# Input projection with high and low halves of the activations in one product, and filler products ahead of the experts

## The reference

```
h = layer_norm(x)
for l in range(2):
    z = h @ w_in[l]                       # 2048 -> 5648, cut into 13 slices
    mix = concat(y_a, y_b, y_c, y_d) @ w_out[l]
    h = layer_norm(alpha * h + mix)
    out = sum over e of combine[:, e] * ((silu(h @ w_gate[e]) * (h @ w_up[e])) @ w_down[e])
    h = layer_norm(alpha * h + out)
```

## Time and profile before

| | |
|---|---|
| median of 3 runs (lowest, highest) | 1715.86 us (1712.81, 1719.31) |
| the profiled execution's own time | 1714.94 us |
| its span, first to last instruction | 1713.2 us |
| mean granted TensorE clock | 0.962 |
| busy: TensorE, VectorE, ScalarE, POOL | 1553.8, 945.7, 546.2, 50.2 us |
| HBM read | 539.88 MB, 316 GB/s over the span |

### The profile page before, as it was taken

One profiled execution on the slowest core, in us unless ns is written; L12 is line 12 of the kernel. 1 busy time (PEld: TensorE's weight loads), 2 busy tenths in 40 slices (PEclk: granted clock), 3 DMA queues, 4 the chain that ended last, 5 costly groups with the idle time before them and its releaser, 6 DMA issues.

```text
span 1713.2 us, 38421 instructions
## 1 busy us (share of the span) xinstructions
PE 1553.8 (91%) x16224; PEld 1090.1 (64%) x16224; DVE 945.7 (55%) x1548; ACT 546.2 (32%) x694; POOL 50.2 (3%) x36
## 2 busy tenths in 40 slices
PE   8999999998899999966599999999997999996664
PEld 8999999884444555422299999998743555452221
DVE  7657655647455556623466476566374556652235
ACT  4553543323222222201265544533321222221112
POOL 0004000000000000000000050000000000000000
PEclk9999999999999999988899999999999999998887
DMA  8655556659999999999965555567589999999996
GB/s 296 216 169 191 170 177 223 244 212 383 420 420 421 420 420 421 420 421 420 396 201 185 165 194 178 162 240 294 235 347 420 420 421 421 421 420 420 421 421 250
DMA packets 138709, 543.88 MB, mean 317 GB/s; under 512 B 23012, under 2 KB 26312, under 8 KB 88536
## 3 DMA queue, kind: packets, MB, share of 16 engines
q1 hardware_dynamic: 138196, 541.97, 81.0%
q10 hardware_dynamic: 388, 0.04, 0.0%
HBM read 539.88 MB, written 2.10 MB: 316 GB/s over the span
## 4 chain that ended last, share of the span: by engine, by line
PE 68%; SPq 15%; DMA 10%; DVE 4%; issue 1%; DVEq 1%; ACT 1%; ACTq 0%
PE ps L826 23%; PE ps L1102 11%; PE ps L988 10%; SPq L408 10%; PE ps L1120 6%; PE ps L823 5%; DMA room<-in_w_up_dram 5%; DMA room<-in_w_down_dram 4%; SPq L412 4%; PE ps L1044 3%; PE ps L1059 3%; PE ps L1079 1%; PE ps L1052 1%; DVE room L1160 1%; DVE w_lo L1160 1%
## 5 line engine op out<-in xcount | busy, mean ns | idle before, releaser
L1102 PE MATMUL ps<-room 128*32 128x256 f32 x5344 | 336.4, 408 | 91.9 <-DMA room<-in_w_up_dram 91.5
L1160 DVE TENSOR_TENSOR w_lo<-room,w_hi 128x2048 fp32r<-128x2048 f32 (+1 forms) x121 | 276.2, 2292 | 228.9 <-ACT w_hi L535 228.4
L1102 PEld LDWEIGHTS ps<-room 128*32 128x32 f32 x5344 | 193.0, 116 | 244.6 <-DMA room<-in_w_up_dram 87.6
L826 PE MATMUL ps<-hT_hi,w_hi 128*128 128x256 f32 x1152 | 329.7, 286 | 1.1 <-DVE w_lo L1160 0.7
L826 PE MATMUL ps<-hT_lo,w_hi 128*128 128x256 f32 x1152 | 326.0, 283 | 0.0
L826 PE MATMUL ps<-hT_hi,w_lo 128*128 128x256 f32 x1152 | 325.9, 283 | 0.0
L535 ACT ACTIVATE w_hi<-room 128x2048 fp32r<-128x2048 f32 x120 | 228.0, 1911 | 228.4 <-PE ps L826 101.7
L1160 DVE TENSOR_TENSOR h<-h,ps 128x512 f32<-128x512 f32 (+1 forms) x380 | 241.7, 698 | 13.7 <-PE ps L1059 13.6
L1160 DVE TENSOR_TENSOR room<-room,ps 128x128 f32<-128x128 f32 (+2 forms) x53 | 18.5, 353 | 400.1 <-ACT room L742 396.7
L826 PEld LDWEIGHTS ps<-hT_hi,w_hi 128*128 128x128 f32 x1152 | 220.9, 192 | 4.7 <-issue 2.4
L826 PEld LDWEIGHTS ps<-hT_hi,w_lo 128*128 128x128 f32 x1152 | 221.0, 192 | 0.7 <-issue 0.5
(11 more groups left out here) (254 smaller groups left out, 1650.0 us busy)
## 6 DMA issues: line engine op xcount, KB each, us to landing
room<-in_w_down_dram SPq DMA_DIRECT2D x116, 1024.0 KB, 22.0
room<-in_w_gate_dram SPq DMA_DIRECT2D x114, 1024.0 KB, 25.3
room<-in_w_up_dram SPq DMA_DIRECT2D x114, 1024.0 KB, 26.8
room<-in_w_in_dram SPq DMA_DIRECT2D x88, 1024.0 KB, 5.0
room<-in_w_out_dram SPq DMA_DIRECT2D x32, 1024.0 KB, 5.2
spare<-in_w_gate_dram SPq DMA_DIRECT2D x14, 1024.0 KB, 24.8
spare<-in_w_up_dram SPq DMA_DIRECT2D x14, 1024.0 KB, 26.7
spare<-in_w_down_dram SPq DMA_DIRECT2D x12, 1024.0 KB, 17.9
```

The lines of the kernel that those rows point to most:

```text
L826: last = eng.matmul(ps[:, b + o // 2, (o % 2) * T:(o % 2) * T + T], w_[:, o * P:o * P + P], x_[:, kk, :], start=opens and o % 2 == 0, stop ...
L1102: last = eng.matmul(ps[r0:r0 + BLK, 0, 0:2 * P], xe[:, x0:x0 + BLK], unit_gu(u)[:, :, k, c * P:c * P + P], start=(i == 0 and k == 0), stop ...
L1160: return eng.tensor_tensor(o, a, b, op)
```

## The change

It has three parts.

1. `hT_hi` and `hT_lo` become two halves of one tensor `hT_parts`. In slabs 1, 3, 4, 5, 7, 8 and 9 (`MERGED`) a high weight block meets both halves in one product of 512 columns, and the low weight block meets `hT_hi` in one of 256. Each column block o has a whole bank: the first 256 words hold high by high and low by high, the other 256 the cross term. The slab thus uses banks 0 to 3.

2. For these slabs `evacuate` is replaced by `copy_cross` on ScalarE (four copies of 256 words, the first three after a column block's last product, the fourth after the slab) and `add_cross` on VectorE (four adds of the bank's first half, each freeing a bank). Where there is a SiLU or GELU, `in_place` applies it after the four adds. Slabs 0, 2, 6 and 10 use banks 0 and 1. The first quarter of a slab waits bank by bank; slabs 1, 3 and 7 take blocks 2 and 3 first. Rounds and splits around these steps change places by one quarter at most.

3. The four fillers in each call of `router` become 12 after the first half's router products, 3 after the second half's transposes and 3 after its router products, and the folding products of both halves move to the end. 3 fillers are put ahead of `turn_rows` and 5 behind it.

```diff
-        hT_hi = part("hT_hi", [P, KD, T], arena_at)
-        hT_lo = part("hT_lo", [P, KD, T], arena_at + 16 * 1024)
+        hT_parts = part("hT_parts", [P, 2, KD, T], arena_at)
+        hT_hi, hT_lo = hT_parts[:, 0], hT_parts[:, 1]
...
+                def copy_cross(s, dst, scale=1.0):
+                    for o in range(4):
+                        if o < 3:
+                            eng.wait_ge(o_done.sem, o_done.at(l, 3 * MERGED.index(s) + o + 1))
+                        else:
+                            eng.wait_ge(w_used.sem, w_used.at(l, 4 * s + 4))
+                        eng.activation(dst[:, o * T:o * T + T], ps[:, o, T:2 * T], ACT.Copy, scale=scale
+                                       ).then_inc(cross_copied.sem, 1)
+
+                def in_place(s, dst, func):
+                    eng.wait_ge(bank_free.sem, freed(l, s))
+                    for i in range(2):
+                        eng.activation(dst[:, i * 512:i * 512 + 512], dst[:, i * 512:i * 512 + 512], func
+                                       ).then_inc(z_evac.sem, 1)
...
+                copy_cross(1, r_x)
                 rounds(11, 12)
-                evacuate(1, r_x)
...
-                rounds(25, 28)
-                evacuate(5, c_g, ACT.Silu)
+                rounds(25, 27)
+                copy_cross(5, c_g)
+                rounds(27, 28)
+                in_place(5, c_g, ACT.Silu)
                 rounds(28, 30)
...
                 eng.activation(a_PT, ps[:, 4:8, 0:384], ACT.Copy).then_inc(att_pTs.sem, 1)
-                rounds(34, 36)
-                evacuate(7, r_g, ACT.Gelu_apprx_tanh)
+                rounds(34, 35)
+                copy_cross(7, r_g)
+                rounds(35, 36)
+                in_place(7, r_g, ACT.Gelu_apprx_tanh)
...
-                    if first == 0 and s >= 2:
-                        eng.wait_ge(z_evac.sem, z_evac.at(l, 2 * (s - 2) + 2))
...
+                        order = (2, 3, 0, 1) if q == 0 and s in (1, 3, 7) else range(2 if token_major else 4)
+                        for ks, o in itertools.product(parts, order):
...
+                            if q == 0 and s:
+                                bank = o if token_major or joined else o // 2
+                                if s in (1, 3, 7) and bank < 2:
+                                    eng.wait_ge(z_evac.sem, evacuated(l, s - 1, bank + 1))
+                                elif s > 1:
+                                    before_it = s - 2 if s in (3, 7) else s - 1
+                                    eng.wait_ge(bank_free.sem, freed(l, before_it, bank))
...
+                                if joined:
+                                    c = slice(o * P, o * P + P)
+                                    eng.matmul(ps[:, o, :], hi[:, c], hT_parts[:, :, kk, :], start=opens, stop=False)
+                                    last = eng.matmul(ps[:, o, 0:T], lo[:, c], hT_hi[:, kk, :], start=False, stop=ends)
+                                    continue
...
                 router(0)
+                keep_busy(12, 7)
                 turn_half(1)
-                router(1).then_inc(logits_done.sem, 1)
+                keep_busy(3, 7)
+                router(1)
+                keep_busy(3, 7)
+                fold_router(0)
+                fold_router(1).then_inc(logits_done.sem, 1)
...
+                keep_busy(3, 2)
                 turn_rows(first_rows.sem, first_rows.at(l, 1), first_turned.sem)
+                keep_busy(5, 2)
...
+                def add_cross(s, dst, scale=1.0):
+                    for o in range(4):
+                        eng.wait_ge(cross_copied.sem, cross_copied.at(l, 4 * MERGED.index(s) + o + 1))
+                        sl = dst[:, o * T:o * T + T]
+                        eng.scalar_tensor_tensor(sl, ps[:, o, 0:T], scale, sl, ALU.mult, ALU.add).then_inc(bank_free.sem, 1)
...
                 splits(10, 11)
+                add_cross(1, r_x)
                 eng.wait_ge(exps_ready.sem, exps_ready.at(l, 1))
...
                     eng.reciprocal(c_rs[:, 512 * i:512 * i + 512], c_rs[:, 512 * i:512 * i + 512])
                     splits(26 + i, 27 + i)
+                    if i == 0:
+                        add_cross(5, c_g)
...
-                splits(32, 37)
-
-                eng.wait_ge(z_evac.sem, z_evac.at(l, 16))
+                splits(32, 35)
+                add_cross(7, r_g)
+                splits(35, 37)
+
+                eng.wait_ge(z_evac.sem, evacuated(l, 7))
...
                 splits(37, 39)
+                add_cross(8, b_c)
                 rest_mix(1, 8)
```

More of the change, by code:

```diff
@@ L270, in trunk, with evacuated, freed @@
         hT_rounded, hT_split = signal("hT_rounded", 5), signal("hT_split", 5)
-        z_evac = signal("z_evac", 2 * (N_IN - 1))
+        z_evac = signal("z_evac", 2 * len(EVACUATED))
+        o_done, cross_copied, bank_free = (signal(n, k * len(MERGED)) for n, k in (
+            ("o_done", 3), ("cross_copied", 4), ("bank_free", 4)))
+        def evacuated(l, s, i=2):
+            return z_evac.at(l, 2 * EVACUATED.index(s) + i)
+        def freed(l, s, o=3):
+            return bank_free.at(l, 4 * MERGED.index(s) + o + 1)
         out_first, res_add = signal("out_first", 1), signal("res_add", 2 * N_OUT)
@@ L649, in _ @@
                 last.then_inc(at_ready.sem, 1)
-                rounds(21, 24)
+                rounds(21, 23)
                 eng.wait_ge(u_ready.sem, u_ready.at(l, 1))
-                evacuate(4, a_kT)
+                copy_cross(4, a_kT)
+                rounds(23, 24)
                 eng.wait_ge(om_ready.sem, om_ready.at(l, 1))
@@ L695, in _ @@
                 rounds(41, 43)
-                evacuate(9, b_h)
+                copy_cross(9, b_h)
                 rounds(43, 47)
@@ L819, in project @@
                                 hi, lo = w_hi[n % 4][:, k, :], w_lo[n % UNITS][:, k, :]
+                                opens, ends = kk == 0, kk == KD - 1
+                                if joined:
[3 more added lines that the diff above has]
+                                    continue
                                 for j, (x_, w_) in enumerate(((hT_hi, hi), (hT_hi, lo), (hT_lo, hi))):
[L821 to L824, removed]
+                                    if token_major:
+                                        last = eng.matmul(ps[:, o, :], x_[:, kk, o * P:o * P + P], w_,
+                                                          start=opens and j == 0, stop=ends and j == 2)
                                     else:
-                                        last = eng.matmul(ps[:, b + o // 2, (o % 2) * T:(o % 2) * T + T],
+                                        last = eng.matmul(ps[:, o // 2, (o % 2) * T:(o % 2) * T + T],
                                                           w_[:, o * P:o * P + P], x_[:, kk, :],
-                                                          start=opens and o % 2 == 0, stop=ends and o % 2 == 1)
+                                                          start=opens and j == 0 and o % 2 == 0,
+                                                          stop=ends and j == 2 and o % 2 == 1)
+                            if joined and q == 3 and o < 3:
+                                last.then_inc(o_done.sem, 1)
                             if between and (q, o) in between:
@@ L921, in _ @@
                 eng.wait_ge(rs_done.sem, rs_done.at(l, 1))
-                eng.wait_ge(z_evac.sem, z_evac.at(l, 10))
+                eng.wait_ge(bank_free.sem, freed(l, 4))
                 qT, kT = blocks(a_qT, 4), blocks(a_kT, 4)
@@ L976, in _ @@
                     if c == 0:
-                        eng.wait_ge(z_evac.sem, z_evac.at(l, 2 * (N_IN - 1)))
+                        eng.wait_ge(bank_free.sem, freed(l, 9))
                     elif c >= 2:
@@ L1336, in _ @@
                     softplus()
-                splits(18, 21)
+                splits(18, 19)
+                add_cross(3, a_qT, float(P) ** -0.5)
+                splits(19, 21)
                 eng.wait_ge(at_ready.sem, at_ready.at(l, 1))
@@ L1417, in _ @@
                 rest_mix(2, 0)
-                splits(41, 44)
-                eng.wait_ge(z_evac.sem, z_evac.at(l, 20))
+                splits(41, 43)
+                add_cross(9, b_h)
+                splits(43, 44)
+                eng.drain()
                 eng.wait_ge(att_o.sem, att_o.at(l, 1))
```

25 lines of the change are left out of this document (15 added, 10 removed).

## The result

| | before | after |
|---|---|---|
| median of 4 runs (lowest, highest) | 1716.78 us (1712.81, 1719.31) | 1774.78 us (1772.23, 1775.92) |
| profiled execution: own time, span | 1714.94, 1713.2 us | 1772.23, 1770.5 us |
| mean granted TensorE clock | 0.962 | 0.947 |
| busy: TensorE, VectorE, ScalarE, POOL | 1553.8, 945.7, 546.2, 50.2 us | 1567.9, 962.4, 553.9, 50.8 us |
| HBM read | 316 GB/s over the span | 306 GB/s over the span |

The change makes the kernel slower: ratio 1.0338, interval 1.0324 to 1.0351. The forecast was 1772 us.

A forecast was written before the change was run, and what follows sets the result against it. TensorE was taken to bound the kernel up to the router, the expert-weight stream after the first gate/up product. 1714.9 + 54.4 - 11.9 - 3.7 + 17.6 = 1771.3, as a median 1772 us; range 1746 to 1787, chance 0.68.

The forecast's parts named there:

- The bound: Projections of both layers: TensorE's own time bounds them, so a microsecond lost or won there is one of the total.
- Rival (4): Expert weight stream: transfers run ahead while TensorE waits and hide the delay; total about 1711 us; chance 0.03.
- The waits: Projections: TensorE waits for banks before slabs 2, 6, 7, 8 and 9; 27.2 us a layer, +54.4 us.
- The two prices taken from the nearest rows: Freeing a bank: VectorE's add of 128x256 at 0.45 us, ScalarE's copy at most 0.53 us.
- The transitions called covered: Slabs 2 to 3, 3 to 4, 4 to 5, 9 to 10: evacuation fits in time; if not, it costs tenths.
- Rival (3): Projections: copies and adds keep ahead of TensorE, only the savings remain; 1699 us, faster; chance 0.05.
- The clock: Behind eight waits of 3 us and more TensorE's clock falls, 2.2 us each: +17.6 us; the 3.1 us wait least certain.
- Rival (1): Projections: the clock holds through the waits; 1754 us; chance 0.14.
- rival (2): Projections: the clock falls longer, 8 x 3.4 us lost instead; 1781 us; chance 0.10.
- The joining: Seven slabs in two layers: 512+256 columns replace 256+256+256, saving 0.213 us a quarter, 56 quarters: -11.9 us.
- The fillers: Router to freed slot: fillers keep the clock up, layer 1 takes what layer 0 takes, -3.7 us; nothing in layer 0.
- rival (5): Router handover: the fillers don't do what they are for, +3.7 us, inside the range; no chance of its own.

The follow-up runs named there:

- the third kernel: Changed kernel with all four late evacuations moved ahead on ScalarE and two slabs' additions ahead of a split on VectorE; 1708.72 us, ratio 0.9961 to the kernel before.
- the filler experiment: Changed kernel plus filler products in TensorE's waits before slabs 2 (10 calls) and 6 (32 calls), waits left in place; 1769.05 us, ratio 1.0311.
- the twin kernels: Two kernels with all four evacuations moved ahead: one keeps joined products, 1708.72 us; the other issues each as two of 256 columns, 1714.73 us.

## Why the prediction was right

**The bound.** TensorE's time in the projections passed to the total as it was, 60.3 us there against 57.3 in all. Rival (4), a stream of weights that hides the delay, did not come: the DMA share fell to 0.54 and 0.53.

**The waits.** This step carried the forecast, and it held place by place:

| before slab | 2 | 6 | 7 | 8 | 9 |
|---|---|---|---|---|---|
| predicted, us a layer | 3.1 | 9.0 | 8.7 | 6.1 | 0.3 |
| layer 0 | 2.85 | 8.97 | 8.75 | 6.15 | 0.1 |
| layer 1 | 3.06 | 8.97 | 8.75 | 6.15 | 0.1 |

The four large ones come to 53.7 us (54.4 were predicted with the small one). Releasers were as named, VectorE's additions and, at slab 7, ScalarE. The two prices taken from the nearest rows erred on the high side: an addition took 0.42 us, not 0.45, and four copies 1.18, under the bound of 0.53 each. The transitions called covered, 2 to 3, 3 to 4, 4 to 5 and 9 to 10, show no wait for a bank. Rival (3) failed on just these four places and is what the third kernel builds: without them the time is 1708.7 us. It was given as 1699; of the missing 9 to 10 us, 3 are the smaller saving of the joined products, 1 the fillers', 4 are small waits, 2 us a layer, and the rest is not accounted for.

**The clock.** Predicted 17.6 us, measured 14.1. The mechanism was right, and the filler experiment shows it apart from the waits; the term was too large because one of eight falls failed to come (the one called least certain) and because a fall cost 2.0 us on average, from 1.6 to 2.6, and not 2.2. Rival (1) put it at nothing and rival (2) at 27.2 us, and it was neither.

**The joining.** This is the term that was mis-sized: -11.9 us predicted, -6.9 measured on the twin kernels. In the changed kernel, the growth of 60.3 us leaves 53.7 + 14.1 - 60.3 = 7.5 for it. The step that failed took the price of a joined product from the output matrix's products of 512 columns, 0.2267 us, and added the 0.120 of the product left over: a pair of 0.3467. The runs show that pair in some stretches and one of 0.353 in the others, and in the twin kernels 2.0 us more of waiting. It looked for one price of the joined form in a row of another product, and the form has two. By the 2.5 ns beyond the columns that the Trainium skill (TensorE: Matmul & The Clock Gate, Back-to-back issue gap) gives, an estimate of the saving is 2.2 us. The 6.9 us of the projections do not agree with it, though they too lie under the prediction's 11.9.

**The fillers.** Predicted -3.7, -2.8 in the profiled executions; rival (5) is out. Layer 1's handover came down to 21.8 us as meant; the prediction overlooked that layer 0's would grow by 0.5, filled where the clock had held anyway.

**The sum.** The missed parts nearly cancel: 53.7 + 14.1 - 6.9 - 2.8 = 58.1 us, and the profiled executions differ by 57.3; predicted were 56.4. Part of that closeness is luck, as joining and clock erred by 5.0 and 3.5 us in opposite directions. What the Trainium skill (TensorE: Matmul & The Clock Gate, HAM oscillation) tells of a kernel in which double-buffering PSUM gave no further gain does not carry over to this one. Here giving up the second pair of banks cost 66 us until the evacuations were moved.

## What to carry to other kernels

When a change makes a step use more buffers, go through every hand-over of those buffers and write down, in program order, what stands ahead of the instruction that frees each; a busy share of 42% (ScalarE) or 58% (VectorE), as in layer 0's projections here, says nothing about it. The repair then is not speed but place: moving four evacuations ahead of work that was not due gave back 66 us where the change had lost 58, and only then did its saving show. Against an idle stretch that can't be removed, fillers saved the loss at half rate where they left 0.6 to 0.8 us idle (before slab 2); where they left 1.83 (before slab 6), they did in one layer of two.

## What was not expected of the hardware

A pair of products, 512 and 256 columns, takes 0.347 or 0.353 us and keeps its pace as long as nothing interrupts the run of pairs, for up to 64 pairs (slab 9, or the second half of slab 3 with the first of slab 4), while the same work as three products of 256 stays at 0.120 each. The pace changes only across an interruption. In the second half of slab 8, layer 0, it was 0.353 in the changed kernel and 0.347 in the one with all evacuations moved, at the same place in the program. What sets it stays open; no run varied it alone.

The clock's answer to a wait is not fixed either. Five kernels wait 2.64 to 3.06 us before slab 2 in both layers: the changed one, the first two with moved evacuations, its unjoined form and the one with the old fillers. Behind eight of these ten waits the clock fell; behind two it did not, in layer 0 of the changed kernel (2.85 us) and of the one with the old fillers (3.04). It can fall late: in layer 1 of the changed kernel TensorE restarted at 942.53 at full rate, and the windows of 2 us show the clock go down a while after:

```profile
942.00:944.00 2.00, 1.47 (x7) 1.25 (x8) 2.00 (x7) 2.00 (x4) 0.00 (x0) 1.00 0.93 353
944.00:946.00 2.00, 2.00 (x6) 1.60 (x5) 2.00 (x3) 0.54 (x1) 0.00 (x0) 0.50 0.00 0
946.00:948.00 2.00, 2.00 (x7) 1.53 (x6) 1.38 (x1) 0.00 (x0) 0.00 (x0) 0.65 0.00 0
```

The price of a short wait is therefore looked for in the products behind it, not only in the wait.
